# Attention on two heads at once in the halves of the array, with the neighbourhood bias added and its row maximum taken by one VectorE instruction

## The reference, cut to what matters

```python
s_c = einsum(qn, k_cmp); p_c = _masked_softmax(s_c, cmp_end <= t); o_c = einsum(p_c, v_cmp)
s_s = einsum(qn, k_g);   p_s = _masked_softmax(s_s, ok);           o_s = einsum(p_s, v_g)
s_w = einsum(qn, k_w);   p_w = _masked_softmax(s_w, ok_w);         o_w = einsum(p_w, v_w)
out = gn[..., 0:1] * o_c + gn[..., 1:2] * o_s + gn[..., 2:3] * o_w
```

## Time and profile before

| | |
|---|---|
| median of 3 runs | 2292.1 us (2281.51 to 2295.62) |
| the profiled execution | 2285.85 us, of which the span is 2283.9 us |
| PE busy | 2201.7 us, 96% of the span |
| DVE busy | 1103.5 us, 48% |
| ACT busy | 852.5 us, 37% |
| GpSimd busy | 237.3 us, 10% |
| mean granted clock of TensorE | 0.983 |
| loads from HBM | 180.82 MB, 80 GB/s |

### The profile page before, as it was taken

How to read it: one execution, slowest core, us unless ns; L and a number is a source line. 1 busy time by engine, 2 the same in 40 slices (tenths; PEclk the granted TensorE clock), 3 DMA queues, 4 the chain that set the end, 5 groups by cost and what they waited for, 6 DMA issues and landing times.

```text
span 2283.9 us, 28971 instructions
## 1 busy us (share of the span) xinstructions
PE 2201.7 (96%) x11040; PEld 1801.1 (79%) x11040; DVE 1103.5 (48%) x1798; ACT 852.5 (37%) x1411; POOL 237.3 (10%) x220
## 2 busy tenths in 40 slices
PE   7998989999999999999999999999999999999997
PEld 5877768888888788889888888876677788888886
DVE  5546555633433736626443445545544445443344
ACT  6324433432323433324332232533476326232232
POOL 2001002010001100310100003401100123000002
PEclk9999988999999999999999999999999999999999
DMA  4223000333222232222332322221111222322331
GB/s 165 90 68 93 19 10 28 102 93 102 92 92 92 93 102 82 86 92 74 102 101 92 94 90 81 84 73 51 34 49 47 83 84 65 111 93 92 100 93 37
DMA packets 52400, 184.51 MB, mean 81 GB/s; under 512 B 5904, under 2 KB 8096, under 8 KB 52288
## 3 DMA queue, kind: packets, MB, share of 16 engines
q1 hardware_dynamic: 49968, 173.39, 24.0%
q0 software_dynamic: 2320, 9.55, 1.3%
HBM read 180.82 MB, written 2.10 MB: 80 GB/s over the span
## 4 chain that ended last, share of the span: by engine, by line
PE 86%; DVE 8%; ACT 3%; POOL 1%; issue 1%; DMA 0%; SPq 0%; ACTq 0%; DVEq 0%; POOLq 0%
PE ps L354 55%; PE ps L941 4%; PE ps L908 3%; PE ps L929 3%; PE ps L1586 3%; PE ps L431 3%; PE ps L1508 3%; PE ps L463 2%; PE ps L919 2%; DVE ring L328 2%; DVE h L553 1%; DVE xa L562 1%; PE ps L1381 1%; ACT ring L321 1%; PE ps L1481 1%
## 5 line engine op out<-in xcount | busy, mean ns | idle before, releaser
L354 PE MATMUL ps<-xa,ring 128*128 128x512 f32 x3192 | 738.9, 391 | 0.0
L354 PEld LDWEIGHTS ps<-xa,ring 128*128 128x128 f32 x3192 | 598.2, 188 | 127.2 <-issue 3.0
L321 ACT ACTIVATE ring<-raw 128x1024 fp32r<-128x1024 f32 x321 | 337.7, 1054 | 513.3 <-PE ps L354 415.8
L328 DVE TENSOR_TENSOR ring<-raw,ring 128x1024 fp32r<-128x1024 f32 x321 | 409.5, 1277 | 245.7 <-ACT ring L321 245.2
L354 PE MATMUL ps<-xb,ring 128*128 128x512 f32 x2208 | 517.2, 395 | 0.0
L354 PEld LDWEIGHTS ps<-xb,ring 128*128 128x128 f32 x2208 | 414.4, 188 | 100.5
L835 DVE TENSOR_TENSOR ffsq<-relu 128x512 f32<-128x512 f32 x96 | 66.3, 691 | 180.3 <-ACT relu L794 180.2
L852 DVE TENSOR_TENSOR acc<-acc,ps 128x512 f32<-128x512 f32 x68 | 46.8, 688 | 207.7 <-PE ps L354 207.7
L941 PE MATMUL ps<-xa,ring 128*128 128x512 f32 x432 | 118.6, 413 | 0.0
L463 PE MATMUL ps<-xa,ring 128*128 128x256 f32 x768 | 97.1, 285 | 11.6 <-POOL xa L740 5.4
L941 PEld LDWEIGHTS ps<-xa,ring 128*128 128x128 f32 x432 | 77.9, 192 | 37.9 <-issue 23.5
(11 more groups left out here) (334 smaller groups left out, 2442.5 us busy)
## 6 DMA issues: line engine op xcount, KB each, us to landing
raw<-in_stream SPq DMA_DIRECT2D x321, 512.0 KB, 3.5
c_w<-in_cmp_w POOLq DMA_DIRECT2D x8, 512.0 KB, 4.2
t<-in_rpb POOLq DMA_DIRECT2D x8, 448.0 KB, 3.6
h<-in_x SPq DMA_DIRECT2D x8, 256.0 KB, 8.4
out_y<-h SPq DMA_DIRECT2D x16, 128.0 KB, 1.9
cons<-in_con SPq DMA_DIRECT2D x1, 738.0 KB, 4.3
wst<-in_w_s POOLq DMA_DIRECT2D x1, 512.0 KB, 4.6
bs<-in_b_s POOLq DMA_DIRECT2D x1, 512.0 KB, 5.3
```

The costliest lines, as they stand in the source:

```text
L321: nc.scalar.activation(ring[:, m % RING, 0], raw[:, m % RING], ACT.Copy).then_inc(hi_done, 1)
L328: nc.vector.tensor_tensor(ring[:, m % RING, 1], raw[:, m % RING], ring[:, m % RING, 0].bitcast(F32), ALU.subtract).then_inc(lo_done, 1)
L354: mm = nc.tensor.matmul(bank[:, :], ring[:, n % RING, w, k * P:(k + 1) * P], operand[:, k, xx], start=(i == 0 and w == 0 and xx == 0), sto ...
```

## The change

Units become pairs: the two heads of a pair are the two halves of the same 128 channels, so the scores of one head use rows 0 to 63 of the array and those of the other rows 64 to 127. Each block of 128 keys is a matmul of its own for each head, head after head, into banks ps4 and ps5. There is one bank of scores for each head of the pair, so the next pair's scores wait for the exponentials (`at_probs`) or, for na, for the maxima (`at_max`). The masks are added in halves as well. The probabilities are scaled by the reciprocal of the sum, and the gate, before they are transposed (`at_norm`); this is in place, 128 partitions by the number of keys. In `pe_values` the values are the weights (64 columns for each head, side by side in the array's columns), the transposed probabilities move, and the result comes out transposed in ps2, with heads in the partitions. sel and win of the same heads are accumulated in the same bank. So `pe_outs` and GpSimd's part fall away after all three attentions: ACT copies a finished bank to the high part, DVE subtracts for the low part. na and swa run in one loop.

For na, the bias is added and the maximum is taken by one `tensor_tensor_reduce`; its result is negated by a small instruction. Four bias tables are kept instead of two. The compressed branch's gate is applied to its probabilities. Some constants move: the masks come in a load of their own, and the memsets of the zero-padded keys are gone, as these keys now need no zeros. The beside work is spread over pairs instead of units.

```diff
+NSA_ORDER = [("sel", 0), ("win", 3), ("sel", 1), ("win", 2), ("sel", 2), ("win", 1), ("sel", 3), ("win", 0)]
+PAIRS = []
+for _p in range(4):
+    for _k, _t in NSA_ORDER:
+        PAIRS.append((_k, _p, _t, 0, (_t + 1) * P))
+U_NA = len(PAIRS)
+for _p in range(4):
+    for _t in range(TB):
+        PAIRS.append(("na", _p, _t, 0, T))
+U_SWA = len(PAIRS)
+for _p in range(4):
+    for _t in range(TB):
+        _lo, _hi = max(0, _t - 1) * P, min(TB, _t + 2) * P
+        PAIRS.append(("swa", _p, _t, _lo, _hi - _lo))
+NU = len(PAIRS)
...
+CMP_AT = {"blocks": 2, "hidden": 3, "gelu": 18, "turn": 19, "copy": 19, "kv": 20, "kv_copy": 20}
+SCORE_AT = (21, 23)
+TURN_AT = (25, 26)
+OUT_AT = (27, 28, 29)
+BLOCK_AT = [2, 2, 3, 3, 4, 4] + [5 + b for b in range(26)]
...
+        def pe_scores(pe, i):
+            kind, p, t, k0, nk = PAIRS[i]
+            if i >= 1:
+                pe.wait_ge(sem("at_max" if PAIRS[i - 1][0] == "na" else "at_probs"), 2 * i)
+            q = {"na": a_q, "swa": w_q}.get(kind, n_q)
+            k = {"sel": n_k[:, 0], "win": n_k[:, 1], "na": a_k[:, p], "swa": w_k[:, 0]}[kind]
...
+                    mm = nc.tensor.matmul(ps[4 + g][:, c * P:(c + 1) * P], q[r, p, t * P:(t + 1) * P],
+                                          k[r, k0 + c * P:k0 + (c + 1) * P], start=True, stop=c not in masks)
+                    if c == last and c not in masks:
+                        mm.then_inc(sem("at_scores"), 1)
+                for w in range(2 if c in masks else 0):
+                    for g, r in enumerate(rows):
+                        mm = nc.tensor.matmul(ps[4 + g][:, c * P:(c + 1) * P], halfb[r, w], masks[c][r, w], start=False,
+                                              stop=w == 1)
+                        if c == last and w == 1:
+                            mm.then_inc(sem("at_scores"), 1)
...
+        def pe_turn(pe, i, probs):
+            for g in range(2):
+                pe.wait_ge(sem("at_norm"), 2 * i + g + 1)
+                if i >= 1:
+                    pe.wait_ge(sem("at_turned"), 2 * i - 1 + g)
+                for j in range(PAIRS[i][4] // P):
+                    mm = nc.tensor.transpose(ps[6 + g][:, j * P:(j + 1) * P], probs[:, i % 2, g, j * P:(j + 1) * P], ident)
+                mm.then_inc(sem("at_turn"), 1)
...
+        def pe_values(pe, i, turned):
+            kind, p, t, k0, nk = PAIRS[i]
+            pe.wait_ge(sem("at_turned"), 2 * i + 2)
...
+                    mm = nc.tensor.matmul(ps[2][r, t * P:(t + 1) * P], v, turned[:, i % 2, g, j * P:(j + 1) * P],
+                                          start=first and j == 0, stop=last and j == nk // P - 1)
...
+                    kind, p, t, k0, nk = PAIRS[i]
+                    for g in range(2):
+                        s = 2 * (i % 4) + g
+                        act.wait_ge(sem("at_max"), 2 * i + g + 1)
+                        if i >= 2:
+                            act.wait_ge(sem("at_turn"), 2 * i - 3 + g)
+                        src = a_s[:, g] if kind == "na" else ps[4 + g][:, 0:nk]
+                        nc.scalar.activation(probs[:, i % 2, g, 0:nk], src, ACT.Exp, bias=stat[:, NMAX, s:s + 1],
+                                             accum_out=stat[:, SUM, s:s + 1]).then_inc(sem("at_probs"), 1)
...
+                        dve.wait_ge(sem("at_scores"), 2 * i + g + 1)
+                        src, dst = ps[4 + g][:, 0:nk], stat[:, NMAX, s + g:s + g + 1]
+                        if kind == "na":
+                            dve.wait_ge(sem("rpb_masked"), 2 * p + g + 1)
+                            dve.wait_ge(sem("at_probs"), 2 * i - 1 + g)
+                            c = (7 - 2 * t - 1) * NA_W
+                            chain(nc.vector.tensor_tensor_reduce(a_s[:, g], src, t2[:, (2 * p + g) % 4, c:c + T], 1.0, NEG,
+                                                                 ALU.add, ALU.max, stat[:, MAX_IN, s + g:s + g + 1]))
+                            nc.vector.tensor_scalar(dst, stat[:, MAX_IN, s + g:s + g + 1], -1.0, None, ALU.mult)\
+                                .then_inc(sem("at_max"), 1)
+                            continue
+                        if kind == "swa":
+                            red = nc.vector.tensor_reduce(stat[:, MAX_IN, s + g:s + g + 1], src, AX.X, ALU.max, negate=True)
+                        else:
+                            nc.vector.tensor_reduce(dst, src, AX.X, ALU.max, negate=True).then_inc(sem("at_max"), 1)
...
+                if i - 3 in ENDS and i - 3 >= first:
+                    out(i - 3, *ENDS[i - 3])
+                beside(i - first)
+                if i < last:
+                    dve.wait_ge(sem("at_probs"), 2 * i + 2)
+                    w = stat[:, SUM, s:s + 2]
+                    if kind == "swa":
+                        dve.wait_ge(sem("at_sink"), i - U_SWA + 1)
+                        chain(nc.vector.tensor_tensor(stat[:, DEN, s:s + 2], w, stat[:, SINK, s:s + 2], ALU.add))
+                        w = stat[:, DEN, s:s + 2]
+                    chain(nc.vector.reciprocal(stat[:, REC, s:s + 2], w))
+                    row = REC
+                        b = 3 * p + (1 if kind == "sel" else 2)
+                        chain(nc.vector.tensor_tensor(stat[:, WGT, s:s + 2], stat[:, REC, s:s + 2],
+                                                      n_gate[:, t, b:b + 13:12], ALU.mult))
+                        row = WGT
+                    for g in range(2):
+                        v = probs[:, i % 2, g, 0:nk]
+                        nc.vector.tensor_scalar(v, v, stat[:, row, s + g:s + g + 1], None, ALU.mult)\
+                            .then_inc(sem("at_norm"), 1)
...
+            def out_heads(kind, p):
+                if kind == "nsa" and p == 3:
+                    nc.scalar.activation(xb[:, 7, 0], ps[2][:, :], ACT.Copy).then_inc(sem("nsa_hi"), 1)
+                elif kind != "nsa":
+                    k = p + (4 if kind == "swa" else 0)
+                    nc.scalar.activation(xb[:, k, 0], ps[2][:, :], ACT.Copy).then_inc(sem("o_hi"), 1)
...
+            def cmp_add(p):
+                dve.wait_ge(sem("cmp_out"), p + 1)
+                dve.wait_ge(sem("at_out"), p + 1)
+                nc.vector.tensor_tensor(xf[:, p], xf[:, p], ps[3][:, :], ALU.add).then_inc(sem("nsa_x"), 1)
...
+            def out_heads(i, kind, p):
+                if kind == "nsa" and p == 3:
+                    dve.wait_ge(sem("nsa_hi"), 4)
+                    nsa_lo(3, ps[2][:, :])
+                elif kind == "nsa":
+                    dve.wait_ge(sem("xlo_ready"), p + 1)
+                    dve.wait_ge(sem("at_values"), i + 1)
+                    nc.vector.tensor_copy(xf[:, p], ps[2][:, :]).then_inc(sem("at_out"), 1)
+                else:
+                    k = p + (4 if kind == "swa" else 0)
+                    dve.wait_ge(sem("o_hi"), k + 1)
+                    nc.vector.tensor_tensor(xb[:, k, 1], ps[2][:, :], xb[:, k, 0].bitcast(F32), ALU.subtract)\
+                        .then_inc(sem("o_lo"), 1)
...
+            dve_attention(dve, chain, U_NA, NU, (a_p, a_pt), beside_na, out_heads)
```

More of the change, by code:

```diff
@@ L902, in pe_scores @@
             if kind == "swa":
                 if t > 0:
[L904 removed]
+                    masks[0] = upb
                 if t < TB - 1:
[L906 to L910 removed]
@@ L945, in pe_blocks, with pe_attention @@
                     mm.then_inc(panel_done, 1)
-        def pe_attention(pe, first, last, probs, turned, beside=None):
+        def pe_attention(pe, first, last, buffers, beside):
             for i in range(first, last + 2):
@@ L961, in act_attention @@
+        NMAX, SUM, SINK, DEN, REC, WGT, SINK_IN, MAX_IN = range(8)
+        def act_attention(act, first, last, buffers, beside, out):
+            probs, turned = buffers
             for i in range(first, last + 2):
                 if i < last:
-                    kind, g, p, t, k0, nk, head = UNITS[i]
-                    s = i % 4
-                    act.wait_ge(sem("at_max"), i + 1)
-                    if i >= 2:
-                        act.wait_ge(sem("at_turn"), i - 1)
-                    src = a_s[:, i % 2, 0:nk] if kind == "na" else ps[4 + i % 2][:, 0:nk]
@@ new lines, in act_attention @@
+                    nk = PAIRS[i - 1][4]
+                    for g in range(2):
+                        act.wait_ge(sem("at_turn"), 2 * i - 1 + g)
+                        if i >= 3:
+                            act.wait_ge(sem("at_values"), i - 2)
+                        nc.scalar.activation(turned[:, (i - 1) % 2, g, 0:nk], ps[6 + g][:, 0:nk], ACT.Copy)\
+                            .then_inc(sem("at_turned"), 1)
+                beside(i - first)
+                if i - 2 in ENDS and i - 2 >= first:
+                    act.wait_ge(sem("at_values"), i - 1)
+                    out(*ENDS[i - 2])
```

429 lines of the change are left out of this document (165 added, 264 removed).

## The result

The changed kernel takes 2208.87 us (median of 4 runs, 2208.43 to 2211.16), the kernel before 2293.32 us in the same comparison (4 runs, 2281.51 to 2295.62): a ratio of 0.9655, 95% interval 0.9626 to 0.9685. In a second comparison it took 2208.74 us against 2285.51 (13 runs), 0.9670 (0.9654 to 0.9686), so that the gain is some 77 us. The profiled execution lasted 2208.62 us, with a span of 2206.9 us against 2283.9.

The account below looks back on a forecast made before the run. TensorE was taken to bound all three attentions, a chain of engines the wait behind `_nsa`. Savings of 14 + 9 + 20 + 8 + 4.7 + 3 = 59 us, less 14 for the clock, gave 2241 profiled, 2247 median, range 2215 to 2283.

Parts of the forecast that it names:

- A step of two heads in 0.11 us: Scores and values: both halves of the array run at once, 0.11 us a step; the other bound was 0.22.
- `_nsa` (-27.3 for -28 with its tail): First attention: 20 us saved in its 32 pairs, and 8 us in the wait behind its last unit.
- swa (-9.5 for -9): swa: VectorE's round bounds at 7.3 us per pair against 7.9 before, over 16 pairs 9 us saved.
- The fused instruction: na, per head: addition and maximum in one instruction, 0.7 us and its reading 0.2, taken as 0.88 us.
- the round with a split: VectorE in 6 of 16 na pairs: a panel's split adds 3.5 us to the round, 7.7 us in all.
- 2.7 over PE's 5.0, 6 x 2.7 = 16 us: na: in six pairs VectorE's round with a split exceeds TensorE's 5.0 us by 2.7, 16 us lost.
- 32 us were saved: na: TensorE's pair falls from 7.0 to 5.0 us, over 16 pairs 32 us, if TensorE stays the bound.
- 14 us lost: All three attentions: mean clock falls to 0.88 to 0.90 as TensorE's share falls to about 0.8, 14 us lost.
- Rival 1: Whole kernel: everything hides and the clock stays, TensorE's savings of 92 us count in full, 2200 us; chance 0.10.
- my case: Whole kernel: the main forecast, 2215 to 2269 us around 2247; chance 0.67.
- Rivals 2 and 3: Halves of the array run one after the other, 2284 us, 0.08; fused instruction slow, 2285 to 2295 us, 0.08.
- rival 4: Three attentions: the clock falls to near 0.7 and the kernel is slower by 44 us, 2336 us; chance 0.07.

Follow-up runs that it names:

- the kernel with both edits: Changed kernel with VectorE's beside work behind the scaling in na and swa only, and constant matmuls at five idle places of `_nsa`: 2187.98 us, ratio 0.9579.

## Why the prediction was wrong, step by step

**Right: the pieces of TensorE.** A step of two heads in 0.11 us was right (eight in 1.03 to 1.09 with the change of tiling; I had 1.03). One count behind it was misread: of the ten instructions in the second row two had begun before it, and eight start, six of them as twos of both heads; it is the spacing of 0.11 us from two to two that carries the step. A pair changes its part of the array three times (values to scores, scores to weights, transposes to values) and not four as the text has it for `_nsa`, and swa's values were charged two changes where na's had one; the sum hangs on neither, as no term used the four and VectorE's round was taken as swa's bound. Right, too, were the pair without a wait (5.27 with 9 matmuls of weights beside; I had 5.0 for the mean of 8.6), `_nsa` (-27.3 for -28 with its tail), swa (-9.5 for -9) and the gate panels (-3.7 for -3). Two of these came out by luck in part. `_nsa` itself was 3.3 us short of its 20 and the tail 2.6 over its 8. In swa the order of the split cost 7.5 us where I had 11, and TensorE's step without it is 6.8 us by that run where I had 6.6; the two errors cancel. The fused instruction was right (0.69, its reading 0.08 for 0.19), and so was the round with a split:

```profile
1546.29 0.69 DVE L1013 CUSTOM_DVE_ANT_0 xf<-ps,t 128x512 f32<-128x512 f32 x1
...
1551.42 1.23 DVE L324 TENSOR_TENSOR ring<-raw,ring 128x1024 fp32r<-128x1024 f32 x1 [2.78 <-ACT ring L317]
...
1553.56 0.69 DVE L1013 CUSTOM_DVE_ANT_0 xf<-ps,t 128x512 f32<-128x512 f32 x1
```

From one fused instruction to that of the next pair it is 7.27 us; I had 7.7. A round without one is 3.65 (1542.64 to 1546.29); I had 4.2.

**Wrong, first: "2.7 over PE's 5.0, 6 x 2.7 = 16 us" in na.** I took the longer of TensorE's step and VectorE's round pair by pair, and added the excesses. But a long round is followed by short ones, and TensorE runs its pairs a step ahead: over the very round of 7.27 us it went on with weights, transposes and values, and only three pairs of na show a wait for the scaling, 1.6 us together. What has to be compared is sums over several pairs: TensorE's 85.2 us against VectorE's 87 to 89 of work and waits for ACT. In swa, where I compared sums, the term came nearer (11 us for 7.5). Moving the split behind the scaling gave 3.8 us in na, which is what the splits really cost; some 12 of the 16 us were wrong.

**Wrong, second: the base from which 32 us were saved.** I reckoned a pair before as 7.0 us from an undisturbed unit and took my savings off the real stretch, but this had 129.4 / 16 = 8.1 us a pair. The groups of TensorE in na before:

```profile
L941 PE MATMUL ps<-xa,ring 128*128 128x512 f32 x138 | 41.1, 424 | 0.0
L908 PE MATMUL ps<-a_k,a_q 64*128 64x512 f32 x64 | 36.6, 655 | 0.8 <-DVE a_v L1093 0.8
L929 PE MATMUL ps<-a_v,a_pt 128*128 128x64 f32 x256 | 33.7, 276 | 0.7 <-DVE a_o L1033 0.7
L919 PE MATMUL ps<-cons,a_p 128*128 128x128 f32 x128 | 19.9, 279 | 3.1 <-ACT a_p L969 3.1
L442 PE MATMUL ps<-cons 128*128 128x256 f32 x12 | 2.9, 379 | 0.0
```

and after:

```profile
L951 PE MATMUL ps<-xa,ring 128*128 128x512 f32 x138 | 36.1, 405 | 0.0
L896 PE MATMUL ps<-a_k,a_q 64*128 64x128 f32 x256 | 18.6, 285 | 2.7 <-DVE stat L1015 1.9 <-DVE a_v L1105 0.8
L934 PE MATMUL ps<-a_pt,a_v 128*64 128x128 f32 x224 | 15.3, 278 | 2.5 <-DVE xb L2287 2.4
L913 PE MATMUL ps<-cons,a_p 128*128 128x128 f32 x120 | 15.7, 274 | 1.6 <-DVE a_p L1048 1.6
```

Busy time counts the overlap of neighbouring groups twice, and some 3.4 us of the last two lie in swa, so this is a guide and no sum. The same 138 matmuls of weights take 5.0 us less; six constant matmuls at the start of na (12 instructions, 2.9 us, line 442), which the change takes out and which my text doesn't mention, are gone; scores and values together save 34 us where I had 30. The kernel before was at half clock in na for a while (0.97), the changed one isn't (1.00). As an estimate, 0.97 over 129.4 us is 7.8 us at half clock, which cost 3.9. With the constants' 2.9 at most that is 6.8, and with the 12.2 us by which the splits were overcharged (16 less 3.8) 19.0 of the 20.8 us that na was better than forecast. The rest is in the smaller terms, the 2 us for the rotary steps among them, and isn't told apart.

**Wrong, third: "14 us lost" by the clock.** I had the clock at 0.88 to 0.90 in all three stretches, with TensorE busy for 0.8 of them. It was busy for 0.90, 0.93 and 0.91, and the clock was 0.90 in `_nsa` and 1.00 and 0.99 in na and swa. In na this error follows from the first: the waits of half a microsecond to two that I deduced from the rounds aren't there. In swa TensorE did wait, 13 times and 10.3 us in all, up to 1.6 us at once, and the clock stayed; there the step from waits to half clock failed by itself. In `_nsa` the fall is real: the part at its start can be mended by about 5 us, the part under the compressed branch's scores came without a wait, and the term of 28 us for that stretch came out with both included.

Together: 20.8 us in na, 14 in the clock, and 6 us of the median of the kernel before, which I added to the profiled execution and which the later, longer comparisons (2285.5 and 2286.1 us) don't have. That is 41 us, against the 38 by which 2247 was too high; the smaller terms erred the other way by the rest. Rival 1, everything hides and the clock stays, was nearer than my case, though not for its reason: VectorE's rounds don't hide by a wide margin, they just fit, as 14.5 us for 15 us of added work show. Rivals 2 and 3 fell by the timelines, rival 4 by the clock.

## What to carry to other kernels

Where engines are coupled through double buffers, compare their work summed over several steps, and only charge a long round when the rounds around it leave no room. Take a saving off a model of the stretch, or scale the model to the stretch first: what is left between the two (constant matmuls, half clock, changes of tiling) may go with the change. An edit that relieves an engine which isn't the bound can measure as nothing alone, and as nearly its full size once the bound has been lowered to that engine: here 0 and 12 us. Where the clock falls, look at what TensorE did just before: a wait can be filled, but a row of short matmuls without a wait needs another remedy.

## What the runs showed of the hardware

Matmuls of 128 columns in float32 (two instructions each in the trace) in the two halves of the array in turn took 0.13 us each (1.03 us for 8), one half after the other 0.19 to 0.2 (1.51 and 1.64 for 8). The instructions of one half start 0.11 us apart whether the other half works or not; that the ratio is 1.5 and not 2 comes from the change of tiling in both, some 0.2 us, and from the instructions that still overlap where one half follows the other.

A scaling of VectorE from SBUF to SBUF (0.44 us for 128x512) that begins while GpSimd works on SBUF ends only behind GpSimd's instruction: two took 2.56 us instead of 0.88 in the kernel with both edits, and 0.95 us with GpSimd's work in short pieces beside them. The fused instruction, which reads PSUM and the table and lasts 0.69 us, took no longer within GpSimd's instruction (at 1502.28 in that kernel); none of its 32 took over 0.70 us in the changed kernel and in the one with both edits. The Trainium skill ("SBUF — State Buffer", SBUF: two separate sides) says that VectorE's two-port modes and GpSimd share a pair of ports that one of them holds for a whole instruction; this trace agrees, with these numbers.

TensorE's granted clock fell to 0.50 under 32 matmul instructions of 64 rows by 32 columns in float32 while TensorE was busy without a stop (2.85 of 2.85 us), and it stayed at 1.00 and 0.99 through na and swa with waits of up to 1.6 us between longer runs of work.
